# Two projections of a transformer stage as rounded high/low products instead of plain fp32, with the index scores spread wider between them

## The reference, cut to what matters

```
aq, ackv, akr, aqi, aki, awi, bq, bk, bv, bf = split_cols(u @ w_in, AB_WIDTHS)
...
o_a = dsa_mixer(aq, ackv, akr, aqi, aki, awi, w_uk, w_uv)   # index scores, top-k of 128 keys, latent attention
o_b = fox_mixer(bq, bk, bv, bf + b_forget)                  # causal attention with forget gates, 8 heads
return concatenate([o_a, o_b]) @ w_out

# inside dsa_mixer, for each block of 128 queries:
rel = relu(einsum('bqhd,bsd->bqhs', qi, k_idx))             # 8 index heads
score = einsum('bqhs,bqh->bqs', rel, wi)                    # weighed and summed over the heads
_, idx = top_k(score, n_keep)                               # n_keep = 128
```

## Time and profile before

| | |
|---|---|
| time, median of 3 runs | 1955.61 us (1954.28 to 1956.35) |
| span of the profiled execution | 1955.5 us |
| PE busy | 1858.7 us (95%) |
| DVE busy | 1013.7 us (52%) |
| ACT busy | 817.2 us (42%) |
| POOL busy | 563.6 us (29%) |

### The profile page before, as it was taken

The page is one execution under the profiler, slowest core; times in us unless marked ns, Lnnn a source line. Parts: engine busy times, 40 slices in busy tenths (PEclk is TensorE's granted clock), DMA queues, the critical chain, the costliest instruction groups (busy, mean ns, idle before and its releaser), DMA issues.

```text
span 1955.5 us, 27379 instructions
## 1 busy us (share of the span) xinstructions
PE 1858.7 (95%) x10570; PEld 1436.1 (73%) x10570; DVE 1013.7 (52%) x2013; ACT 817.2 (42%) x1553; POOL 563.6 (29%) x407
## 2 busy tenths in 40 slices
PE   8999999998878999989999999999999999999998
PEld 7878889832323893457888888889877778888886
DVE  3261452521113625973376676742577625777677
ACT  4223642211102513256455544353366645544543
POOL 3343421011110320046321113233055553123111
PEclk9999999998989999999999999999999999999999
DMA  6232303799999330200233223222203012223321
GB/s 231 99 111 103 130 1 151 302 404 420 420 420 352 125 112 10 86 2 1 87 104 112 86 87 116 103 88 66 44 2 87 2 44 87 86 96 121 128 86 44
DMA packets 86866, 252.05 MB, mean 129 GB/s; under 512 B 12212, under 2 KB 19700, under 8 KB 74448
## 3 DMA queue, kind: packets, MB, share of 16 engines
q1 hardware_dynamic: 81344, 238.79, 33.0%
q0 software_dynamic: 4592, 9.30, 1.3%
q10 hardware_dynamic: 800, 2.20, 0.3%
HBM read 241.89 MB, written 15.73 MB: 132 GB/s over the span
## 4 chain that ended last, share of the span: by engine, by line
PE 49%; DVE 3%; issue 2%; ACT 2%; POOL 0%; DVEq 0%; ACTq 0%; POOLq 0%
PE psA L1572 28%; PE psA L1615 3%; PE psO L1802 2%; PE psT L1802 2%; PE psS L1802 2%; PE psO L2300 2%; PE psT L2350 2%; DVE x L2997 1%; PE psA L1751 1%; PE psS L1615 1%; PE psS L2337 1%; PE psO L1697 1%; PE psA L2337 1%; PE psT L1731 1%; ACT tok L2379 1%
## 5 line engine op out<-in xcount | busy, mean ns | idle before, releaser
L1263 POOL TENSOR_TENSOR w_slot<-ring,w_slot 128x1024 fp32r<-128x1024 f32 (+1 forms) x81 | 213.8, 2658 | 523.5 <-ACT w_slot L2379 523.3
L1572 PE MATMUL psA<-hT_hi,w_slot 128*128 128x512 f32 x960 | 297.7, 389 | 0.0
L2379 ACT ACTIVATE w_slot<-ring 128x1024 fp32r<-128x1024 f32 (+2 forms) x183 | 196.8, 1086 | 162.8 <-DVE ring L2997 75.0
L1572 PEld LDWEIGHTS psA<-hT_hi,w_slot 128*128 128x128 f32 x960 | 180.2, 188 | 37.4
L1572 PE MATMUL psA<-hT_lo,w_slot 128*128 128x512 f32 x480 | 186.7, 389 | 0.0
L2997 DVE TENSOR_TENSOR w_slot<-ring,w_slot 128x1024 fp32r<-128x1024 f32 x98 | 119.9, 1224 | 116.0 <-ACT w_slot L2379 116.0
L2997 DVE TENSOR_TENSOR x<-psA,x 128x512 f32<-128x512 f32 (+1 forms) x186 | 117.1, 662 | 104.2 <-PE psA L1572 68.8
L1572 PE MATMUL psA<-w_slot,hid_part 128*128 128x512 f32 x672 | 161.4, 389 | 0.0
L2379 ACT ACTIVATE scr<-scr,stat 128x384 f32<-128x384 f32 (+3 forms) x224 | 124.4, 556 | 73.9 <-DVE stat L3978 44.1
L2379 ACT ACTIVATE big<-psA 128x512 f32<-128x512 f32 (+5 forms) x135 | 62.1, 483 | 222.7 <-PE psA L1572 122.4
L1572 PEld LDWEIGHTS psA<-w_slot,hid_part 128*128 128x128 f32 x672 | 126.2, 188 | 26.2
(11 more groups left out here) (521 smaller groups left out, 4401.3 us busy)
## 6 DMA issues: line engine op xcount, KB each, us to landing
ring<-in_mlp_w SPq DMA_DIRECT2D x32, 2048.0 KB, 8.1
ring<-in_w_in SPq DMA_DIRECT2D x8, 2048.0 KB, 7.9
ring<-in_w_gate_e SPq DMA_DIRECT2D x14, 1024.0 KB, 17.2
ring<-in_w_up_e SPq DMA_DIRECT2D x14, 1024.0 KB, 21.7
ring<-in_w_down_e SPq DMA_DIRECT2D x13, 1024.0 KB, 27.3
big<-in_w_down_e SPq DMA_DIRECT2D x12, 1024.0 KB, 27.6
ring<-in_ab_w_in SPq DMA_DIRECT2D x5, 2048.0 KB, 9.0
scr<-in_w_down_e SPq DMA_DIRECT2D x7, 1024.0 KB, 25.3
```

The lines of the kernel that those rows point to most:

```text
L1263: nc.gpsimd.tensor_tensor(part(w_lo, c), raw_piece(c), part(w_hi, c).bitcast(F32), ALU.subtract)\
L1572: ins = pe.matmul(o, a, b, start=(at == 1), stop=(at == 3 * len(terms)))
L2379: return nc.scalar.activation(o, i, f, **kw)
```

## The change

`bq` and `bk` become split products. Eight pieces (four each, 128 columns of weights) join `SPLIT` behind `bv`. `second_lo` must now live until `bk` is done, so it moves over `hT` (the subtraction is done in place and waits for `small_projection` of its tile), and `second_hi` moves into ring slot 0, which `aq`, `bv`, `bq` and `bk` then pass over. The slots are then: `ai` 2, `aq` 1, `bv` 2, `bq` 1, `bk` 2, `ao0` 0, `ao1` 1. The high parts of the eight pieces take turns in two places of 1024 words.

ACT rounds the first two pieces behind the last copy of `bv`, ahead of the copies of `turn_small`. It copies out `bq`'s first tile and rounds the third piece ahead of index score 15, and does the rest of the tiles behind the relus, each with one rounding. POOL's list gets the eight matching subtractions. The index scores stand behind two of each three steps (a step is now three rounded products), from step 0 to step 13; the index queries move from `bqT`'s place to `aqT`'s.

```
+INDEX_STEP = 15
...
+    for name in ("bq", "bk"):
+        stage(name, KD, [(m * P, (m + 1) * P) for m in range(4)], name, 0, 1)
...
-        second_hi = over("second_hi", [P, KD, T], "big", a3_at["kh"])
-        second_lo = over("second_lo", [P, KD, T], "big", a3_at["bqT"])
+        rows_slot = ([n for n in turns if n[:-2] not in ("up", "down")].index("ai") + 1) % RING
+        second_hi = over("second_hi", [P, KD, T], "ring", SLOT * rows_slot)
+        second_lo = over("second_lo", [P, KD, T], "hT", 0)
+        pair_w_hi = [over(f"pair_w_hi{i}", [P, KD * P], "big", BIG - 2048 + KD * P * i) for i in range(2)]
...
-        qiT = bqT
+        qiT = aqT
...
+                if n in ("aq", "bv", "bq", "bk") and turn_of % RING == rows_slot:
+                    turn_of += 1
...
             elif c >= SPLIT[c][5] + 2:
                 product(eng, SPLIT[c - 2][4])
+            elif SPLIT[c][0] == "bq":
+                product(eng, SPLIT[SPLIT_AT["bv"] + 1][4])
...
+                if name == "bk":
+                    held[rows_slot] = held[s]
...
-            def feature_major(first, name, some=range(4), between=None):
+            def heads_major(first, name, between=None):
+
+                for m in range(4):
+                    wh, wl = piece(SPLIT_AT[name] + m)
                     o = begin(first + m)
                     for k in range(KD):
-                        ins = pe.matmul(o[:, :], s[:, k * 512 + m * P:k * 512 + (m + 1) * P], hT[:, k, :],
-                                        start=(k == 0), stop=(k == KD - 1))
+                        pe.matmul(o[:, :], wh[:, k, :], second_hi[:, k, :], start=(k == 0), stop=False)
+                        pe.matmul(o[:, :], wh[:, k, :], second_lo[:, k, :], start=False, stop=False)
+                        ins = pe.matmul(o[:, :], wl[:, k, :], second_hi[:, k, :], start=False, stop=(k == KD - 1))
                         if k == KD - 1:
                             ins.then_inc(proj_ready, 1)
                         if between:
                             between(KD * m + k)
...
-                if step < n_index // 2 - 2:
-                    index_pair(2 * step + 4)
+                if step % 3 < 2 and step - step // 3 < n_index // 2 - 2:
+                    index_pair(2 * (step - step // 3) + 4)
...
+            pair_first = SPLIT_AT["bq"]
+            for c in range(2):
+                split_weight(pair_first + c)
             evac(JOBS["turn_small"], kiT)
             evac(JOBS["turn_small"] + 1, krT)
...
+            def pair_queries(m):
+
+                evac(JOBS["bq"] + m, bqT[:, m, :], scale=SCALE)
+                split_weight(pair_first + 2 + m)
+
             for c in range(n_index):
+                if c == INDEX_STEP:
+                    pair_queries(0)
...
-            for m in range(4):
-                evac(JOBS["bq"] + m, bqT[:, m, :], scale=SCALE)
+            for m in range(1, 4):
+                pair_queries(m)
...
             for m in range(4):
                 evac(JOBS["bk"] + m, bkT[:, m, :])
+                if m < 2:
+                    split_weight(pair_first + 6 + m)
...
             def second_low(t):
 
+                dve.wait_ge(ax_ready, t + 1)
                 dve.wait_ge(second_in_hi, t + 1)
```

More of the change, by code:

```diff
@@ L246, in split_pieces @@
         stage(name, KD, halves, name, 0, NT)
+    start = len(pieces)
+    for name in ("bq", "bk"):
+        stage(name, KD, [(m * P, (m + 1) * P) for m in range(4)], name, 0, 1)
     for l, name in enumerate(("ao", "no")):
@@ L493, in build @@
         turns = [n for n, _, _ in weight_plan(w) if n != "experts" and n[:-1] not in ("up1", "down1")]
-        no1_slot = (2 + [n for n in turns if n[:-2] not in ("up", "down")].index("no1")) % RING
+        no1_slot = (4 + [n for n in turns if n[:-2] not in ("up", "down")].index("no1")) % RING
         nsa_q = [over("nsa_q0", [P, 8, T], "ring", SLOT * no1_slot), over("nsa_q1", [P, 8, T], "hT", 0)]
@@ L1078, in part @@
                     return q_w_hi[c % 2].rearrange("p (k n) -> p k n", k=k)
+                if c >= SPLIT_AT["bq"]:
+                    return pair_w_hi[c % 2].rearrange("p (k n) -> p k n", k=k)
                 if c >= SPLIT_AT["ai"]:
@@ L1448, in token_major @@
                         tail(before_norm, t)
-            def feature_major(first, name, some=range(4), between=None):
-                need(name)
-                s = slot(name)
-                for m in some:
+            def heads_major(first, name, between=None):
+                for m in range(4):
+                    wh, wl = piece(SPLIT_AT[name] + m)
                     o = begin(first + m)
                     for k in range(KD):
-                        ins = pe.matmul(o[:, :], s[:, k * 512 + m * P:k * 512 + (m + 1) * P], hT[:, k, :],
-                                        start=(k == 0), stop=(k == KD - 1))
+                        pe.matmul(o[:, :], wh[:, k, :], second_hi[:, k, :], start=(k == 0), stop=False)
+                        pe.matmul(o[:, :], wh[:, k, :], second_lo[:, k, :], start=False, stop=False)
+                        ins = pe.matmul(o[:, :], wl[:, k, :], second_hi[:, k, :], start=False, stop=(k == KD - 1))
                         if k == KD - 1:
@@ L2150, in index_scores @@
             def index_scores(step):
-                if step < n_index // 2 - 2:
-                    index_pair(2 * step + 4)
+                if step % 3 < 2 and step - step // 3 < n_index // 2 - 2:
+                    index_pair(2 * (step - step // 3) + 4)
             for c in (0, 2):
                 index_pair(c)
-            feature_major(JOBS["bq"], "bq", between=index_scores)
+            heads_major(JOBS["bq"], "bq", between=index_scores)
             for j in range(4):
                 turn(JOBS["turn_aq"] + j, [tok[:, t, j * P:(j + 1) * P] for t in range(NT)])
-            feature_major(JOBS["bk"], "bk")
+            heads_major(JOBS["bk"], "bk")
             copied_all(pe, "turn_aq", 4)
```

## The result

The changed kernel took 1965.33 us, the median of four executions (1962.27 to 1965.54); the kernel before beside it 1955.86 (1954.28 to 1956.35). The estimated ratio is 1.0038, with a 95% interval of 1.0026 to 1.005; it isn't the quotient of the two medians, which are 9.5 us or 0.48% apart, and neither are the ratios further down. A time of 1960.5 (0.25% slower) and a range up to 1965.0 had been forecast. The median lies 0.3 us above the range, 4.8 above the forecast. One execution of a later experiment (e11) ran at a granted clock of 0.56 throughout and took 3050.75 us; it is left out of that experiment's times. The profiled execution is the one of 1962.27 (span 1960.4), 4.9 us of span above that of before; the other three stand together at 1965.3 to 1965.5.

A forecast was written before the change was run, and what follows sets the result against it. DVE's top-k, begun after the index sums, was taken to bound the start of `pair_attention`, not PE. Terms 1.85 + 1.2 + 0.4 + 0 + 1.4 = 4.85 us on 1955.6 gave 1960.5 us, range 1957.0 to 1965.0.

The forecast's parts named there:

- The saved time of PE: From `bq` to the pair scores: PE some 10 us shorter, scores issued 8 us sooner, then waiting for DVE.
- PE is the bound: Rival at `pair_attention`: PE, not the top-k, sets its start, so the 8 us count: 1947.6 us; chance 0.05.
- The four delays: Up to the first mask: roundings, pair spacing, held index sums and top-k make the index sums end 3.45 us later.
- the clock at the pair scores: Behind PE's 10 us wait before `pair_attention`: half clock loses 1.3 to 2.8 us of PE's work.
- Two roundings: Ahead of `turn_small`: two roundings on ACT shift everything up to the index pairs by +1.85 us (1.7 to 2.1).
- Spacing: In `bq`: ten index pairs over 14 split steps, with switches, end later by +1.2 us (bounds +0.2 and +2.2).
- POOL's block: At index score 15: POOL's subtraction holds DVE's two-operand index sum, +0.4 us (0 to 1.0).
- Top-k: DVE's top-k beside five POOL subtractions: 0 us added, 48.6 us long as before.
- Start of `pair_attention`: At the first pair scores: half clock after PE's wait, less smaller waits saved, +1.4 us (0 to 2.6).
- transfers: Weight loads into the ring: later starts of `aq`, `bv`, `bq` and `bk` all cost 0.
- the slow clock lasts: Rival in `pair_attention`: PE's clock stays down for 10 us, +2.5 us on the forecast, 1963; chance 0.09.

The follow-up runs named there:

- e11: e7 run again unedited, beside another run of the kernel before: 1950.46 us, ratio 0.9971.
- e7: Changed kernel with `bq`, its index pairs and `turn_aq` moved ahead of `kh` and `vh`, `kh` sums among the top-k steps: 1950.44 us, ratio 0.9969.
- e9: Kernel before (`bq` and `bk` in plain fp32) with the stage order of e7: 1958.38 us, ratio 1.0009.
- e3: Changed kernel with the roundings of `bq` 0 and 1 behind the `turn_small` copies: 1960.92 us, ratio 1.002.
- e4: Changed kernel with `bq`'s first tile copied out and its third piece rounded behind the index sums: 1965.23 us, ratio 1.0036.
- e8: Changed kernel with e4's edit and an index pair behind every one of the first ten `bq` steps: 1963.63 us, ratio 1.004.
- e2: Changed kernel with eleven unread products in PE's idle time ahead of the third pair score: 1963.38 us, ratio 1.0031.
- e10: e7 with the rounding of `bq` 1 behind the forget copy, not ahead of the small transposes: 1952.93 us, ratio 0.9981.
- e1: Changed kernel run again with nothing edited: 1965.67 us, ratio 1.004.
- e5: Changed kernel with three unread products in PE's waits ahead of the third small transpose and of `kh`: 1963.53 us, ratio 1.0035.
- e12: e7 with two unread products in PE's wait ahead of the third small transpose: 1948.74 us, ratio 0.9964.

## Why the prediction was right, and where it fell short

**The chain was read rightly.** The saved time of PE is there: the pair scores are issued 7.4 us sooner by the clock and 7.9 sooner counted from S, against the forecast 8; `bk` takes 812.07 - 789.56 = 22.5 us, against 22.2. Nothing of it reaches the end, since DVE's top-k starts later and takes as long as ever. e7 and e9 are the proof from both sides: with the top-k begun early the rounded products are worth 7 to 8 us (S to X is 194.37 in e9, 187.55 in e7, 186.76 in e11), and without them the early top-k is worth nothing. In e7 DVE's first mask waits for PE, which is the forecast's rival "PE is the bound", brought about by starting the top-k sooner and not by shortening it.

**The four delays and the clock at the pair scores, in the profiled execution.** Two roundings: forecast 1.85, measured 1.51 (S to R; e3 gives all of it back). They took 1.99 us (the earlier trace rows make it 0.98 each and not the 0.95 of the sum), but ACT then made good a part: the first two copies, 0.69 us apart before (727.95 and 728.64), took 1.07 us together after. Spacing and POOL's block: forecast 1.2 + 0.4, measured 1.44 (R to M), of which the block is 0.3 (e4) and the spacing the rest, made up of -1.6 for shorter steps and +2.8 for four bare ones (e8). Top-k: forecast 0, measured -0.1. Start of `pair_attention`: forecast 1.4, measured 1.41 (K to X), with DVE waiting 0.87 us for the third score and 0.88 for the fourth; e2 shows 1.43 of it in the first six pairs. The sum is 4.28 against 4.85; the rest of the 4.9 us of span is a stage that began 0.44 us later and 0.2 behind it. That 4.9 meets 4.85 is so in part luck: the 0.44 were there at ACT's rounding at 653.84 (653.38 before), ahead of all that the change moves. The same distance stands at the rounding of `aq` (670.73 against 670.28) and at those at 693.87 and 705.18 (693.43 and 704.75), and `bq`'s first piece is rounded without a wait, so transfers cost nothing up to there. POOL's subtractions did nothing to `MAX8` and `MATCH_REPLACE8`.

**The Trainium skill's rule** on shared access, "SBUF — State Buffer", section "Who interferes with whom", by which a DVE instruction with two SBUF inputs contends with a GpSimd one that reads SBUF, is now shown for `scalar_tensor_tensor` as well: 2.50 us in place of 0.62 beside a POOL subtraction, and 2.49 in place of 0.48 in e10.

**The step that failed** is "*First, two roundings ahead of `turn_small`*", with its "+1.85 us (1.7 to 2.1)". It priced the wait by its length. PE now stands 1.72 us there, and in the profiles of e1 and e4 its granted clock is at 0.50 for what follows: S to R is 27.42 us in e1 and 27.36 in e4, 4.5 and 4.4 us more than before, where 1.85 were forecast. With it the stage costs 201.34 - 193.59 = 7.75 us in e1, 1.9 of it a longer K to X (0.5 more than in the first profile after). Of the 9.2 us between the spans of e1's profile and of before's, 1.17 are a later begin of the stage and 0.3 lie behind it; between the medians are 9.0, so some 1.3 us of the usual execution are not traced. The forecast had looked at the clock only at the long wait of 10 us, and had used, where the half clock came behind 1.5 us without an instruction, for that place alone. The rival "the slow clock lasts", too, sought the loss there.

What stays open: the same wait of 1.72 us lost the clock in the profiles of e1, e4 and e7 and not in those of after, e2, e8 and e11. Nothing that was read in these traces says which it will be. The times suggest that losing it is the usual case in the changed kernel (three of four executions, and all five of e1, at 1965.2 or more), but only one of these eight was profiled.

## What to carry to other kernels

When an engine gets faster and the time doesn't move, look for the other chain that ends at the same point and for the work at its head; move that work forward, and the saving comes out (e7: 7 us). Before that, price each wait put on PE by more than its length: 1 to 2 us of standing can, in some executions, halve the clock of the 3 to 7 us behind it. And put interleaved work (here the index pairs) as densely as its consumer takes it: a step left bare costs the whole step.

## What the runs showed of the hardware

- A wait of PE of 1.72 us was followed by 1.2 GHz from about 732 to 738.5 in e1, 730.7 to 737.5 in e4 and 728.3 to 731.7 in e7, and by no fall in after, e2, e8 and e11; one of 1.09 us was followed by 742.3 to 745.7 in e10. With the 1.72 filled by unread products the clock stayed at 1.00 in both profiles taken (e5, e12).
- In `pair_attention` a wait of 1.15 us for a mask comes every 10 to 12 us in before, after, e1, e3, e7, e10 and e11, in before at a clock of 1.00 throughout. In e2 (ending at 871.43) and in e10 (at 856.37) one of them was followed by 3 us at 0.50:

```profile
869.97 0.49 PE L1709 MATMUL psS<-big 64*128 64x128 f32 x4 [1.15 <-DVE stat L3832]
```

```profile
871.43 0.49 PE L1723 MATMUL psS<-big 64*128 64x128 f32 x4 [1.15 <-DVE stat L3863]
```

  The first line is of before, the second of e2.
- A rounded-product step, three of 512 columns with a switch to 64-row scores and back, costs 0.90 us; the same step in plain fp32 costs 1.05.
- A `scalar_tensor_tensor` with two SBUF operands is stopped by a POOL subtraction begun before it (2.50 us in place of 0.62 in after, 2.49 in place of 0.48 in e10); `MAX8` and `MATCH_REPLACE8` beside five of them took 48.63 us together, against 48.71 without.
